# RMS norms entered unnormalised: x times weight goes to the matmuls pair by pair, the factor per token is applied to their results

## The reference

```python
def rmsnorm(x, g):
    var = jnp.mean(xf * xf, axis=-1, keepdims=True)
    return (xf * lax.rsqrt(var + RMS_EPS)) * g
...
def short_conv_mixer(h, w_in, w_conv, w_out):
    b, c, v = jnp.split(h @ w_in, 3, axis=-1)
    return (b * causal_dwconv(c * v, w_conv)) @ w_out
...
def conv_ffn(h, w_up, w_conv, w_down):
    g, u = jnp.split(causal_dwconv(h @ w_up, w_conv), 2, axis=-1)
    return (jax.nn.silu(g) * u) @ w_down
...
# first block:  x += short_conv(norm(x)); x += conv_ffn(norm(x)); x += rope attention(norm(x)); x += conv_ffn(norm(x)); x = norm(x)
# second block: x += hybrid_mixer(norm(x)); x += peer_ffn(norm(x)); return norm(x)
```

## Time and profile before

| | |
|---|---|
| median of 3 runs | 1858.62 us (1854.79 to 1858.99) |
| the profiled execution's own time | 1856.62 us |
| its span in the trace | 1854.8 us |
| TensorE busy | 1804.1 us, 97% of the span |
| VectorE busy | 1359.9 us, 73% |
| ScalarE busy | 873.4 us, 47% |
| product with ones and clock-keeping matmuls (L540, L533) | 80 and 152 matmul passes, 18.3 and 37.2 us busy |
| mean granted TensorE clock | 0.995 of full speed |

### The profile page before, as it was taken

One profiled execution on the slowest core, in us unless ns is written; L12 is line 12 of the kernel. 1 busy time (PEld: TensorE's weight loads), 2 busy tenths in 40 slices (PEclk: granted clock), 3 DMA queues, 4 the chain that ended last, 5 costly groups with the idle time before them and its releaser, 6 DMA issues.

```text
span 1854.8 us, 37943 instructions
## 1 busy us (share of the span) xinstructions
PE 1804.1 (97%) x13746; PEld 1685.8 (91%) x13746; DVE 1359.9 (73%) x2435; ACT 873.4 (47%) x1322; POOL 20.5 (1%) x40
## 2 busy tenths in 40 slices
PE   9999999999999999999999999999999999999998
PEld 8999999988999999997899899999999878778886
DVE  5678788855787878355667599977777688885555
ACT  4344334454443465465563454554444344444444
POOL 0000000010000000000100000000000000000000
PEclk9999999999999999999999999999999999999999
DMA  5545654442456545432235345555545455545554
GB/s 208 184 136 180 183 184 153 148 136 69 134 174 189 183 159 205 141 110 69 69 114 182 127 148 170 171 181 171 169 160 169 154 167 177 168 160 184 190 191 136
DMA packets 79852, 292.30 MB, mean 158 GB/s; under 512 B 8912, under 2 KB 9072, under 8 KB 79392
## 3 DMA queue, kind: packets, MB, share of 16 engines
q1 hardware_dynamic: 79056, 287.93, 48.0%
q0 software_dynamic: 720, 3.32, 0.5%
HBM read 290.16 MB, written 1.05 MB: 157 GB/s over the span
## 4 chain that ended last, share of the span: by engine, by line
PE 80%; DVE 15%; ACT 3%; issue 1%; DMA 1%; SPq 0%; DVEq 0%; ACTq 0%
PE ps L499 19%; PE ps L448 18%; PE ps L449 17%; PE ps L450 17%; DVE m L422 4%; PE ps L1828 2%; DVE m L1731 2%; DVE m L1727 1%; PE ps L454 1%; DVE m L603 1%; DMA m<-stream 1%; DVE m L1735 1%; PE ps L540 1%; ACT m L410 1%; PE ps L989 1%
## 5 line engine op out<-in xcount | busy, mean ns | idle before, releaser
L448 PE MATMUL ps<-m,m 128*128 128x256 f32 x3312 | 954.6, 288 | 26.6 <-DVE m L422 11.0
L449 PE MATMUL ps<-m,m 128*128 128x256 f32 x3312 | 938.0, 283 | 0.0
L450 PE MATMUL ps<-m,m 128*128 128x256 f32 x3312 | 937.6, 283 | 0.0
L422 DVE TENSOR_TENSOR m<-m,m 128x1024 fp32r<-128x1024 f32 x542 | 658.1, 1222 | 299.3 <-ACT m L410 297.6
L448 PEld LDWEIGHTS ps<-m,m 128*128 128x128 f32 x3312 | 635.0, 192 | 43.4 <-issue 21.9
L410 ACT ACTIVATE m<-m 128x1024 fp32r<-128x1024 f32 x542 | 570.1, 1052 | 197.4 <-PE ps L450 188.9
L449 PEld LDWEIGHTS ps<-m,m 128*128 128x128 f32 x3312 | 635.7, 192 | 0.8 <-issue 0.2
L450 PEld LDWEIGHTS ps<-m,m 128*128 128x128 f32 x3312 | 635.3, 192 | 0.0
L499 PE MATMUL ps<-m,m 128*128 128x512 f32 x1536 | 364.1, 396 | 2.0 <-DVE m L1926 2.0
L499 PEld LDWEIGHTS ps<-m,m 128*128 128x128 f32 x1536 | 286.8, 188 | 66.1 <-issue 2.1
L1887 ACT ACTIVATE m<-m 128x256 fp32r (+1 forms) x128 | 53.4, 418 | 206.1 <-PE ps L499 198.2
(11 more groups left out here) (250 smaller groups left out, 1162.9 us busy)
## 6 DMA issues: line engine op xcount, KB each, us to landing
m<-stream SPq DMA_DIRECT2D x542, 512.0 KB, 3.3
m<-alibi_t POOLq DMA_DIRECT2D x1, 1536.0 KB, 11.1
m<-con SPq DMA_DIRECT2D x1, 1417.0 KB, 10.5
m<-xT SPq DMA_DIRECT2D x1, 1024.0 KB, 5.0
y<-m SPq DMA_DIRECT2D x4, 256.0 KB, 2.6
m<-wcmpk POOLq DMA_DIRECT2D x1, 512.0 KB, 4.8
m<-wcmpv POOLq DMA_DIRECT2D x1, 512.0 KB, 4.7
m<-fin POOLq DMA_DIRECT2D x1, 512.0 KB, 5.1
```

The costliest lines, as they stand in the source:

```text
L422: nc.vector.tensor_tensor(w_lo[:, r, :], raw[:, r, :], w_hi[:, r, :].bitcast(F32), ALU.subtract)\
L448: nc.tensor.matmul(out, lhs[0], rhs[0], start=start, stop=False, **kw)
L449: nc.tensor.matmul(out, lhs[0], rhs[1], start=False, stop=False, **kw)
L450: return nc.tensor.matmul(out, lhs[1], rhs[0], start=False, stop=stop, **kw)
```

## The change

All norms with a product behind them are done as norm 4 was. `joint_act` and `joint_dve` write the halves of x * weight as soon as a pair of x is added; `first_pe` sums the squares in turn with the first chunk's matmuls; the clock-keeping matmuls behind the sums are gone. The factor is applied to the results: in `sc` to C (squared factor, since C and V both lack it) and to B; in the ffn stages by one more VectorE instruction per step, which scales the g and u tiles from PSUM to SBUF before the convolution; in `qkv` by scaling the cos and sin tables once, and for v by a factor per partition in ScalarE's copy; in `pq` in the copy of the scores. The last two need the factor as a column, which TensorE turns (`r_tok_pe`). For the experts, h itself is still made, beside the query product (`query_dve`, `high_act`, `low_dve`). At the start the parameters and the first chunk are loaded ahead of x, x comes in two halves, and the constants behind chunk 11. `split_pe`, `split_act` and `split_dve` keep their order, apart from shared helpers.

```diff
+    wide = {i: (h_hi, h_lo) for i in range(4)}
+    wide[4] = at(O_OT, KD, T, dt=F32R), at(O_OT + KD * T, KD, T, dt=F32R)
+    wide[5] = at(A0, KD, T, dt=F32R), at(A0 + KD * T, KD, T, dt=F32R)
...
-            if st.s == RING - 1:
+            if st.s == 4 * RING - 1:
                 sp.dma_start(cons[:, :], con).then_inc(s_con, 16)
...
-    def norm_pe(pe, parts):
-
+    def sums_pe(pe, i, k):
+        pe.wait_ge(sq_part, 4 * i + k + 1)
+        for j in (2 * k, 2 * k + 1):
+            ins = nc.tensor.matmul(ps[:, 7, 0:T], ones[:, 0:P], sq[:, j, :], start=(j == 0), stop=(j == 7))
+        if k == 3:
+            ins.then_inc(sum_ready, 1)
+
+    def first_pe(pe, i, slot, out, beside=True):
+
+        hi_, lo_ = wide[i]
         for k in range(4):
-            pe.wait_ge(sq_part, parts + k + 1)
+            if beside:
+                sums_pe(pe, i, k)
+            pe.wait_ge(wide_split, 4 * i + k + 1)
             for j in (2 * k, 2 * k + 1):
-                ins = nc.tensor.matmul(ps[:, 7, 0:T], ones[:, 0:P], sq[:, j, :], start=(j == 0), stop=(j == 7))
-        ins.then_inc(sum_ready, 1)
-        keep_clock_pe(12, 5)
+                ins = exact(out, wt(slot, j), (hi_[:, j, :], lo_[:, j, :]), j == 0, j == KD - 1)
+        ins.then_inc(chunk_done, 1)
+
+    def r_tok_pe(pe, n):
+
+        pe.wait_ge(r_ready, n)
+        for c in range(2):
+            ins = nc.tensor.matmul(ps[:, 3, c:c + 1], rstd[:, c * P:c * P + P], ident[:, 0:1], start=c == 0, stop=c == 1,
+                                   skip_group_check=True)
+        ins.then_inc(rtok_made, 1)
...
+                    slot = arrived(pe, st, *up_at(name, ups + 1, st.s, u))
+                    if st.s == 0 and u == 0:
+                        first_pe(pe, i, slot, bank(0, 0), beside=i > 0)
+                        continue
+                    if st.s == 1 and u == 2:
+                        pe.wait_ge(rms_ready, 1)
+                    up(pe, slot, bank(st.mod(2), u))
+                    if i == 0 and st.s == 0 and u == 1:
+                        for k in range(4):
+                            sums_pe(pe, 0, k)
...
+    def joint_act(act, i, n, last):
+        for k in range(4):
+            act.wait_ge(x_part, 4 * (i - 1) + k + 1)
+            wide_hi_act(act, i, k)
+            square_act(act, k)
+        walk_act(act, Step(last - 1), 1, 0)
+        root_act(act, n)
+
+    def joint_dve(dve, i, last):
+        walk_dve(dve, Step(last - 3), 1, 0)
+        residual_add_dve(dve, i - 1, last, 0)
+        residual_add_dve(dve, i - 1, last, 1)
+        wide_lo_dve(dve, i, 0)
+        residual_add_dve(dve, i - 1, last, 2)
+        wide_lo_dve(dve, i, 1)
+        residual_add_dve(dve, i - 1, last, 3)
+        wide_lo_dve(dve, i, 2)
+        wide_lo_dve(dve, i, 3)
+        walk_dve(dve, Step(last - 2), 1, 0)
+        walk_dve(dve, Step(last - 1), 1, 0)
...
+    def start_act(act):
+        split_hi(act, Step(0), 1, 0)
+        act.wait_ge(s_par, 16)
+        for k in range(4):
+            act.wait_ge(s_x[k // 2], 16)
+            wide_hi_act(act, 0, k)
+        split_hi(act, Step(1), 1, 0)
+        for k in range(4):
+            square_act(act, k)
+        split_hi(act, Step(2), 1, 0)
+        root_act(act, 0)
...
             par = st.mod(2)
-            cg = conv(dve, dc, conv_g, bank(par, 0), wname, st.lin(3, 0))
-            cu = conv(dve, dc, conv_u, bank(par, 1), wname, st.lin(3, NF * 3))
+            nc.vector.tensor_tensor(copied, ps[:, 4 + 2 * par, :].rearrange("p (a t) -> p a t", a=2),
+                                    rstd[:, :].unsqueeze(1).broadcast_to([P, 2, T]), ALU.mult).then_inc(up_scaled, 1)
+            dve.wait_ge(up_scaled, st.lin(1, sems0 + 1))
+            cg = conv(dve, dc, conv_g, copied[:, 0, :], wname, st.lin(3, 0))
+            cu = conv(dve, dc, conv_u, copied[:, 1, :], wname, st.lin(3, NF * 3))
...
         def _(sp):
-            sp.dma_start(x[:, :, :], xT).then_inc(s_x, 16)
             sp.dma_start(tabs[:, :], par).then_inc(s_par, 16)
+            sp.dma_start(raw[:, 0, :], stream[0, :, :]).then_inc(ring_full[0], 16)
+            for h in range(2):
+                sp.dma_start(x[:, 4 * h:4 * h + 4, :], xT[:, 4 * h:4 * h + 4, :]).then_inc(s_x[h], 16)
             stream_all(sp)
```

More of the change, by code:

```diff
@@ L602, in norm_dve @@
-        for k in range(KD):
-            ins = nc.vector.scalar_tensor_tensor(dst[:, k, :], x[:, k, :], par_(weight, k), rstd[:, :],
-                                                 ALU.mult, ALU.mult)
-            ins.then_inc(h_tile if hb is not None else x_normed, 1)
-            if hb is not None and k % 2 and k >= 3:
-                low((k - 3) // 2)
-        if hb is None:
-            dve.wait_ge(x_normed, KD)
-            return
-        low(3)
-        dve.wait_ge(h_part, hb + 4)
-    def wide_hi_act(act, i, g):
-        nc.scalar.activation(wide_hi[:, i, :], x[:, i, :], ACT.Copy, scale=g[:, i:i + 1]).then_inc(wide_high, 1)
@@ new lines, in start_dve, with turn_tables_dve @@
+    def start_dve(dve, dc):
+        split_lo(dve, Step(0), 1, 0)
+        dve.wait_ge(s_par, 16)
+        for k in range(4):
+            dve.wait_ge(s_x[k // 2], 16)
+            wide_lo_dve(dve, 0, k)
+        split_lo(dve, Step(1), 1, 0)
+        split_lo(dve, Step(2), 1, 0)
+        recip_dve(dve, dc, 0)
+        dc.link(nc.vector.tensor_tensor(rope_a, rstd, rstd, ALU.mult))
+    def turn_tables_dve(dve, dc):
+        dve.wait_ge(rms_ready, 3)
+        nc.vector.reciprocal(rstd[:, :], norm_t[:, :]).then_inc(r_ready, 1)
+        dve.wait_ge(s_con, 16)
+        dve.wait_ge(r_ready, 1)
+        o = COFF["cos"]
+        both = cons[:, o:o + 2 * T].rearrange("p (a t) -> p a t", a=2)
+        nc.vector.tensor_tensor(both, both, rstd[:, :].unsqueeze(1).broadcast_to([P, 2, T]), ALU.mult)\
+            .then_inc(rope_scaled, 1)
+        dve.wait_ge(rope_scaled, 1)
@@ L756, in split_dve @@
         for k in range(4):
-            low(k)
+            low_dve(dve, HP[5], k)
         walk(14)
@@ L860, in sc_act, with query_pe @@
         steps(act, None, 0, KD, 6, one)
-    def project_pe(pe, name, n, hb=None):
-        def one(st):
-            g = TC[name]
-            if g + st.s >= 2:
-                pe.wait_ge(tile_copied, st.lin(1, g - 1))
-            up(pe, arrived(pe, st, 1, CH[name]), bank(st.mod(2, 1, g), 0), hwait=hb if st.s == 0 else None)
-        steps(pe, None, 0, n, 6, one, first=1 if hb is not None else 0)
+    def query_pe(pe):
+        g = TC["pq"]
+        for n in range(KD):
+            pe.wait_ge(tile_copied, g + n - 1)
+            r = arrived(pe, Step(n), 1, CH["pq"])
+            if n == 0:
+                first_pe(pe, 5, r, bank(0, 0))
+            else:
+                up(pe, r, bank(n % 2, 0), rhs=wide[5])
+            if n == 3:
+                r_tok_pe(pe, 2)
     def tokens_pe(pe, name, n, skip=0, hwait=None):
@@ L2045, in _ @@
             range_act(act, CH["wo"], CH["ffn1"] - 1)
-            norm_act(act, 3, x_part, 8, HP[3], last=CH["ffn1"])
+            joint_act(act, 3, 3, CH["ffn1"])
             ffn_act(act, "ffn1", NF)
```

242 lines of the change are left out of this document (113 added, 129 removed).

## The result

The changed kernel takes 1835.78 us (median of 4 runs, 1832.61 to 1837.28), the kernel before 1858.8 beside it: a ratio of 0.9874, 95% interval 0.986 to 0.9888. Two further series of the same kernel gave 1833.93 and 1835.56 us. The forecast was 1832, its range 1826 to 1841. The total came out, but not by the terms that were forecast: two fell short (the start and norm 6) and an unforeseen one made up for them, which is luck.

The account below looks back on a forecast made before the run. TensorE sets the end and loses time at the seams, in serial chains before the product. 28.6 us saved less 2.1 and 1.0 added, net 25.5, takes 1856.6 to 1831.1; 1832 was put for the median, range 1826 to 1841.

Parts of the forecast that it names:

- the start: Norm 0 and the loads: chunk 3 would start at 22.5, before at 27.85; 5.3 us saved.
- norm 6: First chunk behind norm 6 done at 1030.25, before 1034.8; 4.55 us saved.
- The seams: Norms 1, 2 and 3: sums run among the first chunk's matmuls; 5.75, 5.8 and 7.2 us saved.
- Rival 4: Seams joined but paced by ScalarE's halves and squares, gaining little: 15 us in all, 1841 us; chance 0.05.
- rival 2: Root and reciprocal behind the first chunk come too late; each seam gives back 1 to 3 us, 1835 to 1841; chance 0.10.
- The lower bound of 3.5: Least saving in us claimed at the start, if the loads come 2 us later.
- a fall of the clock at a seam: TensorE idle at a seam drops to 1.2 GHz, up to 6.3 us more, once or several times: 1835 to 1845; chance 0.06.
- its own last paragraph: Wrong if VectorE's wait vanishes, granted clock is under 1.00 at a seam, or low halves delay a stage's second to fourth chunk.
- D: Start of the last down chunk before a norm; first chunk ends forecast near D + 9.9 at norms 1 and 2.
- The added work: Scaling in the ffn stages adds 2.1 us and turning the factor into a column 1.0 us.
- the four terms: Uncovered scaling at the start and end of each ffn stage: 4 x 0.52 = 2.1 us; 40 steps cost nothing.
- the two turns of the factor: Small float32 products on TensorE making the factor a column, twice: 0.5 us each, 1.0 in all.

Follow-up runs that it names:

- the second execution of the changed kernel: The changed kernel run once more with nothing edited; 1833.93 us, ratio 0.987 to the kernel before.
- the padded kernel before: The kernel before with two unused columns taken, so every tile behind them lies 32 bytes further; 1854.57 us against 1859.11, ratio 0.9976.
- Without the layout: The changed kernel with r_tok taken behind norm_t and rstd, which lie where they lay in the kernel before; 1838.85 us, ratio 0.9894.

## Why the prediction was right, and where it was not

**The seams: right in mechanism and size.** After ScalarE's first high half the chunk is done in 7.95 us at norms 1, 2 and 3 (forecast 7.8), bound by TensorE with one short wait. They saved 18.95 us, forecast 18.75. Rival 4 (seams gain little) did not happen, nor did rival 2: at the four joined seams TensorE waits for no low half in the second to fourth chunk. Making the chunk wait for the root gives back 10.4 us of the 21.9 saved at the four seams.

**The start: the step that failed.** "The halves of x at 5.9 and 7.1" rests on 0.41 MB per us, which the two rows cited don't give: 1810 KB between 5.77 and 10.62 are 0.37, and one half of x, 512 KB, takes 1.25 us even at 0.41, not the 0.9 between 5.0 and 5.9. The larger error is that one rate was used for the whole start, though the loads moved 0.17 MB per us from 4 to 6 us: x was awaited until 8.6 to 9.4, TensorE's first pass came at 10.5 to 11.5 and not at 8.5. That is 2 to 3 us, and 0 to 1.9 more for the clock in the idle time that it left. The term was 5.3 and measured 0.6 in the first execution, 27.85 - 24.85 = 3.0 in the second. The lower bound of 3.5, worked out for loads 2 us late, did not hold either. The chain behind the first pass was right: 14.0 us to the fourth chunk in the forecast, 14.14 measured at full clock, with the wait ahead of that chunk at 1.20 (forecast 1.5).

**The clock: a rival dismissed too cheaply.** I gave a fall of the clock at a seam 0.06, on the strength of one row, 3.69 us idle at granted clock 1.00. The Trainium skill, "TensorE: Matmul & The Clock Gate", section "HAM oscillation — how this bites in real kernels", warns of bursts that start at half clock behind an idle time. The runs bear it out at norm 6 in each of ten executions (1.4 to 3.0 us lost), and at the start in nine of ten. The one row was itself the exception: in all 13 other traces of this case the same idle time of 3.69 us is followed by the lower clock. There the 32 products, 3.84 us in the earlier trace rows, took 5.46 in the second execution of the changed kernel (first line), and 6.21 in the padded kernel before, which differs from that of the earlier trace rows only in where data lie (second line):

```profile
1445.32 5.46 PE L496 MATMUL ps<-m,m 128*128 128x128 f32 x32 [3.69 <-DVE m L2002]
1464.80 6.21 PE L490 MATMUL ps<-m,m 128*128 128x128 f32 x32 [3.69 <-DVE m L1926]
```

A second trace of the kernel before would likely have shown it. By its own last paragraph the prediction is wrong where the granted clock is under 1.00 at a seam, and at norm 6 it was. The other signs came as forecast: chunk 9.7 us after D (9.9), the multiplication 0.68 us, VectorE's wait for L416 in a step of `ffn0` down from 1.42 to 0.83 (0.9), the waits at the ends of the ffn stages 1.57 (1.5).

Norm 6 saved 2.95 and would have saved about 4.45 at full clock, beside the forecast 4.55.

**The added work: right.** The ffn stages cost 1.45 and 0.6 by the two traces, 1.8 by the waits of the run without scaling (forecast 2.1). The 1.45 are not the scaling alone: 0.54 at the end and 0.5 at the beginning are, the other 0.4 are the weight chunk that landed late there. The first wait of `ffn1` grew by only 0.11 (0.74 to 0.85), so that the four terms are not the equal 0.52 of the sum; the two turns of the factor 0.6 and 0.4 (forecast 1.0).

**A term that was missing.** The change takes two columns for r_tok, and with them shifts norm_t and rstd by 32 bytes. The experts' down stage, whose second pair of weights lies over them, gets 5.0 to 5.4 us shorter. This has nothing to do with norms, and no view of the trace of before pointed to it but that one: 393 ns a matmul where 389 are possible. Together: 18.95 + 2.95 + 0.6 + 5.4 saved, 2.05 + 1.0 added by the ffn stages and the turns, 24.9 net. The two profiled executions are 19.3 apart, because the changed one lost 3.7 us to the lower clock between 720 and 1010 and 1.6 behind the idle time near 1450, where the profiled execution of the kernel before, unlike the others, did not; the medians are 23.0 apart. Without the layout the kernel takes 1838.85 us: nearly 7 above the forecast and above the forecast's own range of 1827 to 1837, though inside the wider one up to 1841. That the median came within 4 us of 1832 is luck to that extent.

## What to carry to other kernels

A factor that is constant along the contraction can be multiplied in behind the product; what it can buy at each seam is the part of the serial chain that stood between sums and product (here 6 us of 12.7), and what it costs is only what stands at a pipeline's fill and drain. Whenever an edit takes or frees on-chip memory, compare the pace of stages that it doesn't touch: an unused pad in the kernel before shows in one run how much of a gain is layout. And a gap of some 3.5 us on TensorE should be priced with the passes behind it at 1.2 GHz, and filled with no more unread work than the gap is long. One trace in which the clock stays up behind a gap proves little; look at the same gap in a second one.
